# Projecting both halves of v tile by tile, and moving decays, late modulation and weight splits to other steps

## The chip, the cores and the metric

The kernel runs on one NeuronCore of a Trainium2 chip. Its time is in device microseconds (us) for one execution; lower is better. The core has a matmul engine (TensorE, PE in the profile, PEld for its weight loads), VectorE (DVE), ScalarE (ACT), GpSimd (POOL) and a queue engine (SP) that issues most DMA transfers. Every engine executes its own list of instructions in order; semaphores tie the lists together. The matmul engine has two clock levels, 1.2 and 2.4 GHz; the profile gives the granted clock as a share of 2.4 GHz.

## The reference

One layer of a diffusion backbone over 1024 latent tokens and 256 context tokens of width 1024, in float32:

```
sx1, cx1, gx1, sx2, cx2, gx2 = split(silu(c) @ w_mod + b_mod, 6)       # same for the context's first two
hx = rmsnorm(x, norm1) * (1 + cx1) + sx1                                # hc from ctx likewise
u, q, k, v, g, r = split(h @ w_in, [512, 256, 256, 512, 512, 32])       # one projection
lg = log_sigmoid(r @ w_gk2 + b_gk) / 16                                 # per key channel, two directions
o  = chunked gated linear attention(q, k, v, lg), forward + backward, state carried from context
y  = concat(box-window pooling of u @ w_pool, rmsnorm(o) * silu(g)) @ w_out
x  = x + gx1 * y
x  = x + gx2 * moe(rmsnorm(x, norm2) * (1 + cx2) + sx2)                 # 16 experts, top 2, grouped router
return rmsnorm(x, norm_f)
```

The change is in the part that makes u, q, k, v, g and lg; the arithmetic stays as it is.

## The kernel before, in words

Tokens are ten tiles of 128 (tiles 0 to 7 latent, 8 and 9 context). Each float32 matmul of the projection is done as three: every operand is split into a high part (rounded by ScalarE, `part_high`, L659, for weights, `hx_high`, L653, for tokens) and a low part (the difference, by VectorE, `part_low`, L915, and `hx_low`, L911), and high x high, high x low and low x high are summed in PSUM, 24 matmuls for a group (8 blocks of 128 of the width, three products).

The projection is a list of 54 groups, `groups`; all engines walk it in the same loop over n, each doing its share of step n. Before: groups 0 to 9 are v's first 256 columns for tiles 0 to 9, groups 10 to 19 its second 256 columns, 20 to 27 are u, 28 to 33 k, 34 to 37 q, 38 to 45 g's first half, and 46 to 53 g's second half, which run later beside the attention state. The weights are eight parts of 256 columns (m = 0, 1 for v, 2, 3 for u, 4 for k, 5 for q, 6, 7 for g), each with two pieces that are split one after the other. There are two places for a raw part (`raw_part`), one for a high part (`high_part`) and two for a low part (`low_part`). `piece_free` says after which group a piece may be overwritten, `pieces_at` in which step the splits stand.

What TensorE does in step n, in this order: the group (`proj`, L1428 for v and g, L1431 for u, k and q), the eight transposes of tile n+2 (`turn_rows`, L1355), at three steps the low-rank gate projection of several tiles (`rank_rows`, L1401, in `R_STEPS`), the logits of tile n-10 (`logits`, L1446), and the cumulation of the decays of tile n-13 (`cumulate`, L1456). Some steps begin with a matmul against a row of ones (`late_turn`, L1465).

Around it, in step n: ScalarE and VectorE scale the transposed tile n+2 out of PSUM, half each (`hx_out`, L646 and L905), then evacuate group n-1; ScalarE squares rows of a later tile (L632) and does the exponentials and logarithms of the decays (L669 to L684); VectorE scales rows (L898) and does the softplus (L978). The groups of v go in turn to ScalarE (L700) and VectorE (L1029); u and g go to ScalarE, k and q to VectorE (L1038, L1041), multiplied into the decays. v uses two PSUM banks, the other groups four; logits use banks 2 and 3 as the transposes do, so u's groups with four banks wait for softplus.

The late modulation (the four of six vectors that are not needed for hx: 32 quarters of 512 KB of w_mod) is summed on VectorE (`late_sum`, L951 and L953) at the steps in `QUARTERS`; a load goes out when the sum two before it is done. After four quarters TensorE adds over partitions (`late_turn`) and VectorE adds the bias and hands a row of 512 on (`late_row`, L966). The next row's first sum waits for that matmul. SP issues the loads of weight parts and quarters in one written order; a load whose wait is not met holds all behind it.

From step 31 on VectorE also runs the box-window pooling of u (`pool_steps`, L988 to L1019), 32 parts: three a step through step 37, then one a step, and what is left after the loop. Then the state steps of the attention start (L1100, matmuls L1498).

After the loop: state steps with g's second half, scores and output projection, router, and 23 to 24 blocks of the experts (L1644), whose first weight loads wait for the last output projections.

Of the kernel before, what the change touches and what calls it, by code (L numbers as in the profile page):

```python
# [50 lines left out]
LAG_L, LAG_C = 10, 13  # L51
R_STEPS = {3: (0, 4), 7: (4, 4), 9: (8, 2)}
HC = HALF // 2
QUARTERS = ([10 + q for q in range(10)] + [20 + q // 2 for q in range(16)] + [28 + q for q in range(6)])
# [20 lines left out]
def hybrid_block(nc, x, c, ctx_in, c_ctx, w_mod, b_mod, norm1, norm2, w_in, w_gk2, b_gk, w_pool,  # L75
                 pool_scale, gla_gain, w_out, w_router, router_bias, w1, w3, w2, norm_f, inv_counts, out):
    with ExitStack() as stack:
# [47 lines left out]
        ROWS = NT - 1  # L125
        rows_at = [O_Q + t * D for t in range(ROWS)] + [O_V + NX * HALF]
        assert O_Q + ROWS * D == O_V
# [4 lines left out]
        with nc.sbuf_tensor("lead_u", [P, O_U], F32), nc.sbuf_tensor("rank_w", [P, KC, RANK2], F32) as w_r:  # L132
            pass
        sq0 = at(O_U + 256, None, D)
# [130 lines left out]
        groups = ([("v", h, t) for h in range(2) for t in range(NT)] + [("u", p, g) for p in range(NG) for g in range(2)]  # L265
                  + [("k", a, 2) for a in range(2)] + [("k", a, g) for a in range(2) for g in range(2)]
                  + [("q", a, g) for a in range(2) for g in range(2)] + [("g", h, t) for h in range(2) for t in range(NX)])
        NV = 2 * NT
        PB = 4

        def bank_of(n):

            return n % 2 if n < NV else n % PB

        def bank_before(n):

            if n < NV + 2:
                return n - 2
            return {NV + 2: -1, NV + 3: -1}.get(n, n - PB)
# [27 lines left out]

        def piece_free(m, i):

            if by_rows(m) and by_rows(m - 1):  # L310
                return (S["half_used"], m // 4 + 1) if i == 0 else (S["proj_done"], part_end[m - 1])
            if by_rows(m) or by_rows(m - 1):
                return S["proj_done"], part_end[m - 1]
# [3 lines left out]
        for m in range(1, len(parts)):  # L317
            for i in range(2):
                last = part_end[m - 1] if by_rows(m) or by_rows(m - 1) else block_end(m - 1, i)
                pieces_at.setdefault(last - 1, []).append((m, i))  # L320
# [5 lines left out]
        for n, g in enumerate(groups):  # L326
            on_act = g[0] in "ug" or (g[0] == "v" and g[2] % 2 == 0)
# [6 lines left out]
        group_no = {g: n for n, g in enumerate(groups)}  # L334
# [60 lines left out]
        def _(sp):  # L395
# [7 lines left out]
            def load_part(m):  # L403
                if m >= 2:
                    sp.wait_ge(S["proj_done"], part_end[m - 2])
                col = parts[m][1]
                sp.dma_start(raw_part[m % 2].rearrange("p (k n) -> p k n", k=KC), win_v[:, :, col:col + HC]).then_inc(part_loaded[m % 2], 16)
# [15 lines left out]
            for t in range(2, NT):  # L423
                load_rows(t)
            load_part(1)
            for q in range(len(QUARTERS)):
                for m in range(2, 6):
                    if q == {2: 2, 3: 12, 4: 19, 5: 27}[m]:
# [1292 lines left out]
```

## Time and profile before

| | |
|---|---|
| median of 3 runs | 1045.63 us (1043.37 to 1046.85) |
| profiled execution, its own time | 1045.96 us |
| its span, first to last instruction | 1044.2 us |
| mean granted clock of TensorE | 0.929 |
| busy: TensorE, its weight loads | 88%, 71% |
| busy: VectorE, ScalarE, GpSimd | 59%, 37%, 18% |
| stage of the change | about 38 to 320 us of the span |
| instructions | 15159 |

### The profile page before, as it was taken

Reading aid. Unit: us, or ns where it says so; the run is one execution under the profiler, and the core shown is the slowest. Engines: PE = TensorE matmul, PEld = TensorE weight load, DVE = VectorE, ACT = ScalarE, POOL = GpSimd, SP = SyncE. Lnnn points to the kernel's source line nnn. Section 1 sums busy time; section 2 is a strip of 40 time slices with the busy share of each in tenths; the row PEclk is TensorE's granted clock in tenths of the full one; section 3 lists DMA queues with packets and bytes.
Section 4 is the critical chain, followed back from the end, with each engine's and each line's share of the span. In section 5 each row is a group of like instructions: output and inputs, shape, how many; then the busy total and the mean of one; then the engine's idle time right before and its main releaser. Section 6 shows DMA issues by size and latency. Waiting matters only on the chain. (4 is left out here: it accounts for less than half of the span.)

```text
span 1044.2 us, 15159 instructions
## 1 busy us (share of the span) xinstructions
PE 917.3 (88%) x5471; PEld 736.8 (71%) x5472; DVE 616.0 (59%) x814; ACT 388.5 (37%) x525; POOL 189.4 (18%) x210
## 2 busy tenths in 40 slices
PE   3788998899878999999973899999999999999960
PEld 1578776677677845656543788889888888988860
DVE  0554533557995634454436654949975467499933
ACT  1654453210012231212114153737754345477613
POOL 4110000000000001000100122323342232234322
PEclk8888998999989989999995699999999999999985
DMA  9800424552111362111156658898998886699928
GB/s 335 325 2 1 123 88 128 176 180 73 51 41 33 133 239 81 57 65 41 41 193 230 252 147 244 264 323 249 371 380 260 243 266 204 186 339 381 333 38 344
DMA packets 81136, 194.73 MB, mean 186 GB/s; under 512 B 3893, under 2 KB 12218, under 8 KB 81098
## 3 DMA queue, kind: packets, MB, share of 16 engines
q1 hardware_dynamic: 68736, 152.05, 41.4%
q0 software_dynamic: 7616, 25.34, 9.9%
q10 hardware_dynamic: 4746, 16.82, 4.2%
q8 instruction: 25, 0.41, 0.2%
q14 instruction: 13, 0.11, 0.0%
HBM read 168.50 MB, written 25.71 MB: 186 GB/s over the span
## 5 line engine op out<-in xcount | busy, mean ns | idle before, releaser
L1568 PE MATMUL ps<-arena 128*128 128x512 f32 x256 | 113.3, 595 | 0.0
L1644 PE MATMUL ps<-w3h,xTh 128*128 128x256 f32 x368 | 105.9, 288 | 0.0
L1428 PE MATMUL ps<-high,hx_h 128*128 128x256 f32 x288 | 89.0, 309 | 18.7 <-DVE low_even L915 6.7
L1644 PE MATMUL ps<-w3h,xTl 128*128 128x256 f32 x368 | 104.2, 283 | 0.0
L1644 PE MATMUL ps<-w3l,xTh 128*128 128x256 f32 x368 | 104.1, 283 | 0.0
L1428 PE MATMUL ps<-high,hx_l 128*128 128x256 f32 x288 | 85.8, 298 | 0.0
L1568 PEld LDWEIGHTS ps<-arena 128*128 128x128 f32 x256 | 47.4, 190 | 54.4 <-issue 53.6
L1279 DVE TENSOR_TENSOR w1l<-raw,w1h 128x2048 fp32r<-128x2048 f32 x30 | 68.6, 2287 | 29.0 <-ACT w1h L811 29.0
L811 ACT ACTIVATE w1h<-raw 128x2048 fp32r (+1 forms) x32 | 61.1, 1913 | 58.4 <-PE ps L1644 39.4
L1644 PE MATMUL ps<-w2h,hTh 128*128 128x512 f32 x184 | 76.9, 418 | 1.3 <-DVE hTl L1292 0.9
L1428 PEld LDWEIGHTS ps<-high,hx_h 128*128 128x128 f32 x288 | 60.0, 208 | 25.5 <-issue 11.7
L1644 PE MATMUL ps<-w1h,xTh 128*128 128x512 f32 x184 | 72.7, 395 | 3.4 <-DVE xTl L1272 3.4
L1644 PE MATMUL ps<-w1l,xTh 128*128 128x512 f32 x184 | 72.5, 394 | 0.0
L1644 PE MATMUL ps<-w1h,xTl 128*128 128x512 f32 x184 | 72.3, 393 | 0.0
L1644 PE MATMUL ps<-w2l,hTh 128*128 128x512 f32 x184 | 72.2, 392 | 0.0
L1644 PE MATMUL ps<-w2h,hTl 128*128 128x512 f32 x184 | 72.1, 392 | 0.0
L811 ACT ACTIVATE w2h<-raw 128x2048 fp32r (+1 forms) x32 | 61.1, 1918 | 28.9 <-PE ps L1644 21.1
L1279 DVE TENSOR_TENSOR w2l<-raw,w2h 128x2048 fp32r<-128x2048 f32 x32 | 71.7, 2283 | 0.0
L1644 PEld LDWEIGHTS ps<-w3l,xTh 128*128 128x128 f32 x368 | 70.5, 192 | 0.9
L1644 PEld LDWEIGHTS ps<-w3h,xTh 128*128 128x128 f32 x368 | 70.4, 191 | 0.9
L1279 DVE TENSOR_TENSOR w3l<-raw,w3h 128x2048 fp32r<-128x2048 f32 x31 | 70.9, 2286 | 0.0
L1644 PEld LDWEIGHTS ps<-w3h,xTl 128*128 128x128 f32 x368 | 70.5, 192 | 0.0
(259 smaller groups left out, 1961.9 us busy)
## 6 DMA issues: line engine op xcount, KB each, us to landing
raw<-in_w_dram SPq DMA_DIRECT2D x48, 2048.0 KB, 13.5
arena<-in_w_mod_dram SPq DMA_DIRECT2D x32, 512.0 KB, 3.7
arena<-in_w_mod_dram SPq DMA_DIRECT2D x4, 2048.0 KB, 16.0
arena<-in_w_in_dram SPq DMA_DIRECT2D x8, 1024.0 KB, 5.4
x_rows<-arena ACTq DMA_DIRECT2D x9, 512.0 KB, 2.6
hx_rows<-arena ACTq DMA_DIRECT2D x9, 512.0 KB, 2.6
arena<-in_x_dram SPq DMA_DIRECT2D x8, 512.0 KB, 12.6
arena<-in_w_out_dram SPq DMA_DIRECT2D x2, 2048.0 KB, 8.3
```

The lines of the kernel that those rows point to most:

```text
L811: act.activation(half_of(j, w_hi[j][:, :], k), half_of(j, raw[:, bass.ds(base, UNIT)], k), ACT.Copy).then_inc(w_high[j], 1)
L1279: dve.tensor_tensor(half_of(j, w_lo[j][:, :], k), half_of(j, raw[:, bass.ds(base, UNIT)], k), half_of(j, w_hi[j][:, :], k).bitcast(F32), A ...
L1428: ins = pe.matmul(out_ap, hx[x_][:, t, k, :], w[w_][:, k, :], start=(k == 0 and i == 0), stop=(k == KC - 1 and i == 2))
L1568: ins = pe.matmul(ps[:, 5 + h, :], m, w[:, k, :], start=(k == 0), stop=(k == KC - 1))
L1644: ins = pe.matmul(out_ap, parts[l][:, lhs], w_parts[w][:, cols], start=start and n == 0, stop=stop and n == 2)
```

## The change

- v's groups run tile by tile: group 2t is the first half of tile t, group 2t+1 the second. The high part of v's second weights has its own place (`high_v1`, over what is later part of the queries' decays), so both are split before the loop; one for q's weights too (`high_q`), and a third place for raw weights is used for u's first part.
- The transposes of tile t+2 stand behind group 2t (tile 2's behind group 1). Scaling, squares and rows move with them. All of v is evacuated by ScalarE.
- Logits stand at steps 15 to 24, cumulations at 17 to 26 (before 10 to 19 and 13 to 22); rank matmuls behind groups 7, 15 and 18.
- Late modulation: one quarter a step from 4 to 19, two a step from 20 to 27, none later; `late_turn` stands behind the step's group (8, 12, 16, 20, 22, 24, 26, 28) and `late_row` at the end of VectorE's step.
- v and u together use two banks, k, q and g four. Pooling starts at step 30. The splits of g's first part stand in step 35, in q, and VectorE's splits stand ahead of its sums and its pooling.
- SP: rows 2, v's second part, rows 3 to 9, the last two each behind a transpose, then quarters with u's and k's parts among them, then q's and g's.

```diff
--- before.py
+++ after.py
...
 COL_U, COL_Q, COL_V, COL_G, COL_R = 0, HALF, HALF + 2 * QK, 2 * HALF + 2 * QK, 3 * HALF + 2 * QK
-LAG_L, LAG_C = 10, 13
-R_STEPS = {3: (0, 4), 7: (4, 4), 9: (8, 2)}
+LAG_L, LAG_C = 15, 17
+R_STEPS = {7: (0, 4), 15: (4, 4), 18: (8, 2)}
 HC = HALF // 2
-QUARTERS = ([10 + q for q in range(10)] + [20 + q // 2 for q in range(16)] + [28 + q for q in range(6)])
+QUARTERS = ([4 + q for q in range(16)] + [20 + q // 2 for q in range(16)])
 MID = P // 2
...
-        ROWS = NT - 1
-        rows_at = [O_Q + t * D for t in range(ROWS)] + [O_V + NX * HALF]
-        assert O_Q + ROWS * D == O_V
+        rows_at = [O_K + 3 * D, O_K + 4 * D, O_Q, O_Q + D, O_K, O_K + D, O_K + 2 * D, O_V + NX * HALF]
+        rows_at += rows_at[0:2]
+        assert O_K + 5 * D == O_V
         rows = [at(off, None, D) for off in rows_at]
             pass
+        with nc.sbuf_tensor("lead_v1", [P, O_Q + 4 * HALF], F32), nc.sbuf_tensor("high_v1", [P, PART], F32R) as high_v1:
+            pass
+        with nc.sbuf_tensor("lead_q", [P, O_G], F32), nc.sbuf_tensor("high_q", [P, PART], F32R) as high_q:
+            pass
+        raw_u0 = at(O_U + 256, None, PART)
+        high_of = {1: high_v1, 5: high_q}
         sq0 = at(O_U + 256, None, D)
...
         FIN_GROUPS = [(0, 1), (1, 1), (2, 2), (4, 2), (6, 2)]
-        groups = ([("v", h, t) for h in range(2) for t in range(NT)] + [("u", p, g) for p in range(NG) for g in range(2)]
+        groups = ([("v", h, t) for t in range(NT) for h in range(2)] + [("u", p, g) for p in range(NG) for g in range(2)]
                   + [("k", a, 2) for a in range(2)] + [("k", a, g) for a in range(2) for g in range(2)]
         NV = 2 * NT
+        group_no = {g: n for n, g in enumerate(groups)}
         PB = 4
+        RING = NV + 2 * NG
-            return n % 2 if n < NV else n % PB
+            return n % 2 if n < RING else n % PB
-            if n < NV + 2:
-                return n - 2
-            return {NV + 2: -1, NV + 3: -1}.get(n, n - PB)
+            return n - 2 if n < RING + 2 else {RING + 2: -1, RING + 3: -1}.get(n, n - PB)
...
+        def high_for(m):
+
+            return high_of.get(m, high_part)
+
+        def raw_for(m):
+
+            return raw_u0 if m == 2 else raw_part[m % 2]
+
         def piece_free(m, i):
-            if by_rows(m) and by_rows(m - 1):
-                return (S["half_used"], m // 4 + 1) if i == 0 else (S["proj_done"], part_end[m - 1])
-            if by_rows(m) or by_rows(m - 1):
-                return S["proj_done"], part_end[m - 1]
+            if m == 7:
+                return (S["half_used"], 1) if i == 0 else (S["proj_done"], part_end[6])
+            if m in (2, 6):
+                return S["proj_done"], part_end[m - 2]
+            if m == 5:
+                return S["proj_done"], group_no[("k", 1, 0)]
             return S["proj_done"], block_end(m - 1, i)
         pieces_at = {}
-        for m in range(1, len(parts)):
+        for m in range(2, len(parts)):
             for i in range(2):
-                last = part_end[m - 1] if by_rows(m) or by_rows(m - 1) else block_end(m - 1, i)
-                pieces_at.setdefault(last - 1, []).append((m, i))
+                step = {2: part_end[0] - 1, 5: group_no[("k", 1, 0)] + i, 6: group_no[("q", 0, 1)], 7: part_end[6] - 1}.get(m)
+                pieces_at.setdefault(block_end(m - 1, i) - 1 if step is None else step, []).append((m, i))
+
+        turn_after = {1: 2, **{2 * (t - 2): t for t in range(3, NT)}}
+        hx_at = {n + 1: t for n, t in turn_after.items()}
+        scale_at = {2 * (t - 2) - 1: t for t in range(3, NT)}
+        square_at = {2 * (t - 2) - 3: t for t in range(4, NT)}
         for n, g in enumerate(groups):
-            on_act = g[0] in "ug" or (g[0] == "v" and g[2] % 2 == 0)
+            on_act = g[0] in "ugv"
             if on_act:
                 evac[n] = ("ev_v", nv)
-        group_no = {g: n for n, g in enumerate(groups)}
...
             def load_part(m):
-                if m >= 2:
+                if m == 2:
+                    sp.wait_ge(S["mod_turned"], 1)
+                    sp.wait_ge(S["ss_ready"], NT)
+                elif m >= 3:
                     sp.wait_ge(S["proj_done"], part_end[m - 2])
                 col = parts[m][1]
-                sp.dma_start(raw_part[m % 2].rearrange("p (k n) -> p k n", k=KC), win_v[:, :, col:col + HC]).then_inc(part_loaded[m % 2], 16)
+                sp.dma_start(raw_for(m).rearrange("p (k n) -> p k n", k=KC), win_v[:, :, col:col + HC]).then_inc(part_loaded[m % 2], 16)
...
             load_part(0)
-            for t in range(2, NT):
+            load_rows(2)
+            load_part(1)
+            for t in range(3, NT):
+                if t >= 8:
+                    sp.wait_ge(S["turned"], t - 7)
                 load_rows(t)
-            load_part(1)
             for q in range(len(QUARTERS)):
-                for m in range(2, 6):
-                    if q == {2: 2, 3: 12, 4: 19, 5: 27}[m]:
+                for m in range(2, 5):
+                    if q == {2: 11, 3: 18, 4: 26}[m]:
                         load_part(m)
                 load_late(q)
+            load_part(5)
             load_part(6)
...
                 act.wait_ge(part_loaded[m % 2], 16 * (m // 2 + 1))
-                if m >= 1:
+                if m >= 2:
                     act.wait_ge(*piece_free(m, i))
-                act.activation(piece(high_part[:, :], m, i), piece(raw_part[m % 2], m, i), ACT.Copy).then_inc(S["part_high"], 1)
+                act.activation(piece(high_for(m)[:, :], m, i), piece(raw_for(m), m, i), ACT.Copy).then_inc(S["part_high"], 1)
...
                 elif g[0] == "u":
+                    if g[1:] == (2, 0):
+                        act.wait_ge(S["lg_done"], NT)
                     out_ap, func = uT[:, g[1], g[2] * HALF:(g[2] + 1) * HALF], ACT.Copy
...
             part_high(0, 1)
-            square(2)
             hx_out(1)
             hx_high(1)
+            square(2)
+            part_high(1, 0)
+            part_high(1, 1)
             square(3)
             for n in range(group_no[("g", 1, 0)]):
-                if n + 2 < NT:
-                    hx_out(n + 2)
+                if n in hx_at:
+                    hx_out(hx_at[n])
                 if n >= 1:
                     evacuate(n - 1)
-                if n + 2 < NT:
-                    hx_high(n + 2)
-                if n + 4 < NT:
-                    square(n + 4)
+                if n in hx_at:
+                    hx_high(hx_at[n])
+                if n in square_at:
+                    square(square_at[n])
                 if 0 <= n - LAG_C - 1 < NT:
...
                 dve.wait_ge(S["part_high"], 2 * m + i + 1)
-                dve.tensor_tensor(piece(low_part[m % 2][:, :], m, i), piece(raw_part[m % 2], m, i),
-                                  piece(high_part[:, :], m, i).bitcast(F32), ALU.subtract).then_inc(S["part_split"], 1)
+                dve.tensor_tensor(piece(low_part[m % 2][:, :], m, i), piece(raw_for(m), m, i),
+                                  piece(high_for(m)[:, :], m, i).bitcast(F32), ALU.subtract).then_inc(S["part_split"], 1)
...
             part_low(0, 1)
-            scale_rows(2)
             hx_out(1)
             hx_low(1)
+            part_low(1, 0)
+            part_low(1, 1)
+            scale_rows(2)
             sc = ("s_chain", [0])
...
                 for c in range(count):
-                    dve.tensor_copy(rT[0:32, (first + c) * P:(first + c + 1) * P], ps[RANK2 * c:RANK2 * (c + 1), 6, 0:P])\
+                    dve.tensor_copy(rT[0:32, (first + c) * P:(first + c + 1) * P], ps[RANK2 * c:RANK2 * (c + 1), 4, 0:P])\
                         .then_inc(S["rT_ready"], 1)
...
             pooling = pool_steps()
-            pool_from = group_no[("k", 1, 2)] + 2
+            pool_from = group_no[("k", 1, 2)] + 1
             for n in range(group_no[("g", 1, 0)]):
-                if n + 2 < NT:
-                    hx_out(n + 2)
+                if n in hx_at:
+                    hx_out(hx_at[n])
                 if n - 1 in R_STEPS:
                     evacuate(n - 1)
-                if n + 3 < NT:
-                    scale_rows(n + 3)
-                if n + 2 < NT:
-                    hx_low(n + 2)
+                if n in scale_at:
+                    scale_rows(scale_at[n])
+                if n in hx_at:
+                    hx_low(hx_at[n])
                 if 0 <= n - LAG_C < NT:
                     softplus(n - LAG_C)
-                if n - 1 in late_turn_at:
-                    late_row(late_turn_at[n - 1])
+                for m, i in pieces_at.get(n, ()):
+                    part_low(m, i)
                 for q, at_step in enumerate(QUARTERS):
                         next(pooling, None)
-                for m, i in pieces_at.get(n, ()):
-                    part_low(m, i)
+                if n - 1 in late_turn_at:
+                    late_row(late_turn_at[n - 1])
             for _ in pooling:
...
-                if n == 3:
+                if n == 7:
                     pe.wait_ge(S["rw_loaded"], 16)
...
                         for c in range(count):
-                            ins = pe.matmul(ps[RANK2 * c:RANK2 * (c + 1), 6, 0:P], w_r[:, k, :],
+                            ins = pe.matmul(ps[RANK2 * c:RANK2 * (c + 1), 4, 0:P], w_r[:, k, :],
                                             hx[part][:, first + c, k, :].bitcast(F32), start=(k == 0 and part == 0),
...
                 elif n >= NV:
-                    pe.wait_ge(S["sp_ready"], n - NV + 7)
-                w = [p_[:, :].rearrange("p (k n) -> p k n", k=KC) for p_ in (high_part, low_part[m % 2])]
+                    pe.wait_ge(S["sp_ready"], NT)
+                w = [p_[:, :].rearrange("p (k n) -> p k n", k=KC) for p_ in (high_for(m), low_part[m % 2])]
                 if g[0] == "v" and g[1] == 0:
...
                                             start=(k == 0 and i == 0), stop=(k == KC - 1 and i == 2))
-                    if k == 3 and n + 1 == part_end[m] and m in (0, 6):
+                    if k == 3 and n + 1 == part_end[m] and m == 6:
                         ins.then_inc(S["half_used"], 1)
...
             for n in range(group_no[("g", 1, 0)]):
+                proj(n)
+                if n in turn_after:
+                    turn_rows(turn_after[n])
                 if n in late_turn_at:
                     late_turn(late_turn_at[n])
-                proj(n)
-                if n + 2 < NT:
-                    turn_rows(n + 2)
                 if n in R_STEPS:
```

## Rows read from the trace of the kernel before

**Rows 1.** The page, busy us, share of the span, instructions.

```profile
PE 917.3 (88%) x5471; PEld 736.8 (71%) x5472; DVE 616.0 (59%) x814; ACT 388.5 (37%) x525; POOL 189.4 (18%) x210
```

**Rows 2.** Stretches: us, length, TensorE busy (instructions), mean clock, DMA share, GB/s.

```profile
45.60:98.20 52.60, 41.07 (x480) 0.87 0.06 20
98.20:104.20 6.00, 6.00 (x56) 1.00 0.00 0
104.20:165.80 61.60, 53.17 (x375) 0.97 0.41 120
165.80:203.50 37.70, 37.65 (x158) 0.91 0.44 134
203.50:266.00 62.50, 52.40 (x226) 0.94 0.45 139
266.00:289.10 23.10, 23.09 (x96) 0.95 0.04 12
289.10:320.20 31.10, 24.45 (x192) 0.89 0.11 35
320.20:335.40 15.20, 11.19 (x94) 0.89 0.00 0
```

**Rows 3.** TensorE's waits: line, releaser, us, times, longest; four stretches in turn.

```profile
PE ps L1428 <- DVE arena L1029: 6.6, 3, 3.1
PE ps L1428 <- ACT arena L700: 3.9, 2, 1.9
PE ps L1428 <- DVE hx_l L911: 1.1, 1, 1.1
...
PE ps L1446 <- DVE arena L978: 8.5, 4, 4.9
...
PE ps L1465 <- DVEq L958: 10.1, 4, 3.3
...
PE ps L1428 <- DVE low_even L915: 6.7, 1, 6.7
PE ps L1498 <- DVE state L1100: 2.5, 1, 2.5
```

**Rows 4.** Timeline around 40 to 45 us: start, duration, engine, instruction, count.

```profile
40.21 1.22 DVE L915 TENSOR_TENSOR low_even<-arena,high 128x1024 fp32r<-128x1024 f32 x1
...
42.81 1.36 DVE L905 TENSOR_SCALAR hx_f<-ps,a,mod 128x128 f32<-128x128 f32 x4
...
41.06 1.50 ACT L646 ACTIVATE hx_f<-ps,mod,a 128x128 f32<-128x128 f32 x4
...
44.47 1.04 PE L1355 MATMUL ps<-ident,arena 128*128 128x128 f32 x8
```

**Rows 5.** Groups by line, 38 to 170 us: count, busy us, mean ns, idle before.

```profile
L953 DVE SCALAR_TENSOR_TENSOR wp<-arena,silu_c,wp 128x512 f32<-128x512 f32 x21 | 15.7, 748 | 0.7 <-DVE wp L953 0.2
...
L659 ACT ACTIVATE high<-arena 128x1024 fp32r<-128x1024 f32 x5 | 5.2, 1049 | 1.5 <-PE ps L1428 1.5
```

**Rows 6.** Groups by line of VectorE, 237 to 330 us: the pooling.

```profile
L995 DVE TENSOR_TENSOR arena<-arena 128x1024 f32<-128x1024 f32 (+6 forms) x10 | 15.3, 1531 | 0.5 <-DVE wp L953 0.2
L1011 DVE TENSOR_TENSOR arena<-arena 128x1024 f32<-128x1024 f32 (+6 forms) x10 | 13.0, 1300 | 0.4
...
L1004 DVE TENSOR_TENSOR arena<-arena,icnt 128x1024 f32<-128x1024 f32 x4 | 4.9, 1226 | 0.1
```

**Rows 7.** Stretch 260 to 300: busy PE, PEld, DVE, ACT, POOL, then clock and DMA.

```profile
260.00:300.00 40.00, 30.04 (x128) 23.72 (x127) 38.12 (x49) 4.34 (x4) 1.41 (x2) 0.87 0.19 60
```

**Rows 8.** Timeline of VectorE: the first state step.

```profile
328.16 1.13 DVE L1100 TENSOR_SCALAR state<-ps,dec 128x128 f32<-128x128 f32 x4
```

**Rows 9.** DMA issues: count, size of one, median us from issue to landing.

```profile
arena<-in_w_mod_dram SPq DMA_DIRECT2D x32, 512.0 KB, 3.7
arena<-in_w_mod_dram SPq DMA_DIRECT2D x4, 2048.0 KB, 16.0
arena<-in_w_in_dram SPq DMA_DIRECT2D x8, 1024.0 KB, 5.4
```

## The prediction

> **What bounds the kernel now.** I read the page's busy line first: TensorE is busy 88% of the span and no other engine over 60% [rows 1]. So what can shrink is TensorE's idle time and the time it runs at the lower clock. The diff touches only the projection loop, some 45 to 320 us, so next comes the table of stretches of that loop. In it the reader is to see that the first stretch (v's first half, 45.6 to 98.2) is busy 41.1 of 52.6 us at a mean clock of 0.87, and that the stretch of g's first half (289 to 320) is busy 24.5 of 31.1 us; the clean row is the second: two groups of v in 6.0 us at clock 1.00 [rows 2]. Third come TensorE's waits: 11.6 us in v's first half, all between a tile's transposes and the next group; 8.5 us for softplus in v's second half; 10.1 us for the late modulation sum in u and k; 6.7 us for the weights of g; 2.5 us for the first state step [rows 3]. Together 39.4 us.
>
> The clock takes the rest. A row's mean clock is a mix of 1.2 and 2.4 GHz; one minus it, times the busy time, is about what the lower level cost. Over the stretches without the clean one [rows 2]: 0.13 x 41.1 = 5.3; 0.03 x 53.2 = 1.6; 0.09 x 37.7 = 3.4; 0.06 x 52.4 = 3.1; 0.05 x 23.1 = 1.2; 0.11 x 24.5 = 2.7; 0.11 x 11.2 = 1.2. Sum 18.5 us.
>
> So 57.9 us of this loop and of the first state step are not matmul at full clock. TensorE's instructions stay the same in number and shape, so the change can win only from these 57.9 us, and it must be charged with each new wait. What comes after needs all tokens (router, then experts), and the experts' first loads wait for the last output projections, so I pass all of it on to the end.
>
> **Part by part.** I follow the new order by durations of one operation: a v group 3.0 us [rows 2], a u, k or q group of 512 columns 5.6 us (four in 23.1 us at clock 0.95), a tile's eight transposes 1.0 us [rows 4], a split into high 1.05 us on ScalarE and into low 1.2 us on VectorE, one step of a late sum 0.75 us, so 1.5 us for a quarter [rows 4, 5].
>
> *Transposes two tiles ahead, two groups a tile.* Before, transposes of tile t+2 were followed at once by the group that needed, through its bank, ScalarE's or VectorE's evacuation queued behind the scaling of that same tile. Now after the transposes of a tile come one group, two at most, that need nothing of it. Scaling (1.5 us, ScalarE) [rows 4] and the short evacuation behind it end some 2 us after the transposes, the next group takes 3.0: the 11.6 us go, with a margin of 1 us. VectorE's budget is tighter: per tile 1.4 (its half of the scaling), under 1.2 for the rows, 1.2 (low part), two quarters of a late sum 3.0, so at most 6.8 us against TensorE's 3.0 + 3.0 + 1.0 = 7.0. What hides it is that a tile's scaling is due only 6 us after its transposes end. At groups 8, 12 and 16 the sum waits for TensorE's own row of ones, which puts VectorE 2.5 us back; I take 0.2 us for that. With its cover gone it costs what is over: 1 us a tile.
>
> *Price of it at the start.* Group 1 now needs v's second half of the weights. VectorE ends the first half at 41.4, then scales tile 1 (1.4, to 42.8); ScalarE makes its high part (1.1, to 43.9), squares tile 2 (1.2, a pass like a split and a short read), splits the weights (1.05, to 46.1); VectorE subtracts (1.2): 47.3. TensorE ends group 0 at 44.6 [rows 4], so 2.7 us of waiting. All seven waits of 2.5 us or more that I followed on the timeline had a spell of the lower clock behind them; I charge 1.5 us a spell (5.3 us over the four spells of v's first half, rounded up) [rows 2, 3]. Sum 4.2.
>
> *Decays run in u.* Logits of a tile are now two steps ahead of its softplus and VectorE has no evacuation of v before it, so the softplus is ready a group earlier: 3.6 of the 8.5 us go. The other 4.9 us stood before u, where the splits of u's weights waited for the last v group. Now u's weights need only the first half's last group: one v group, the rank matmuls and some decays lie over 2 x 1.05 + 1.2 us. They go. In return five logits and seven cumulations of decays run between u groups; the count is the same. SP's queue: v's second half is now ahead of seven row loads (1 MB, some 3 us), hidden, since row 3 is due about 50 us; rows 8 and 9 wait for transposes 0 and 1, done by 40 us. u's first load comes between late quarters 10 and 11, with four groups before it is due, against 5.4 us of landing [rows 9].
>
> *Late modulation ahead of k.* A quarter's load is issued when the sum two before it is done, and lands in 3.7 us [rows 9]: a pair of quarters needs 5.2 us, two v groups take 6 to 7, a u step 7. It holds. TensorE's matmul for a row stands after the group instead of ahead of it, which gives VectorE 5.6 us more. In u I find each row ready 0.5 to 2.5 us before TensorE comes. The last is not: between u's last group and the row at group 28 lie 1.05 + 1.2 (k's second piece), two quarters 3.0 and the row's own add 0.7, in all some 6.2 with handoffs, under a group of 3.0. A wait of 3.2 us, and a spell of clock 1.5: 4.7 charged, of the 10.1 us that go.
>
> *Extra places.* g's weights are split during q (its load is issued after the last k group, 5.4 + 2 x 1.05 + 2 x 1.2 = 10 us, against 22 of q). The 6.7 us go. But VectorE: pooling's parts now start one step earlier, 24 of 32 by the end of q instead of 21. The operations of pooling sum to some 50 us (15.3 + 13.0 + 3 x 4.9, three lines being alike, and some 7 of copies, memsets and chaining) [rows 6], of which 39 are now due before q's last evacuation, with nine evacuations (11) and four splits (4.8): 55.2 us from the end of group 29. TensorE does eight groups (44.8) and three of g (8.7), then wants that bank: at 53.5. A wait of 1.7 us, and half a spell: 2.5. If TensorE is slower elsewhere this wait shrinks; if VectorE's chain is 5% longer it is 4.5.
>
> *First state step.* VectorE began it at 328.2, some 7.7 us after group 45, with three parts of pooling (5.2 us) behind the last split [rows 8]. Now one part (2.5 us) is left, so it starts 2.7 us sooner: the 2.5 us go, to the last tenth.
>
> **The sum.** 57.9 removed; added 4.2 + 0.2 + 4.7 + 2.5 = 11.6; 46.3 us. I keep back 3 us for handoffs where I found under 1.5 us of margin (some eight places). So 43 us from the profiled execution's 1045.96: 1003 us. That execution lies 0.3 us above the median shown (1045.63), which I ignore.
>
> From both sides: the new waits could be nil (the 11.6 and the 3 come back: 988) or, by the nearest rows, each as long as the longest of its kind (4.9 for VectorE, 6.7 for the weights, 3.3 for the sum, with spells: 19): 1011.
>
> One rule of the Trainium skill speaks against the change. u had four PSUM banks and now has two. The trace has v in two banks with no wait between groups and clock 1.00 in the clean stretch [rows 2]. *TensorE: Matmul & The Clock Gate*, section "A second HAM failure mode: psum-queue depth-cycling", says that cycling through PSUM banks leaves micro-idles that make the clock swing between its two levels. By the row it costs nothing. By the rule the clock of the whole loop would stay as it was, which is the rival below.
>
> **Rivals.**
> A. The clock stays low in v and u though the waits go. For: v's first half lost 5.3 us to the clock though, by the longest of each kind, its waits were mostly under 2 us [rows 2, 3]. Against: 1.00 in the clean row. Then only 0 to 4 of the 18.5 us come back: 1003 + 15 to 18 = 1018 to 1021.
> B. VectorE becomes the bound in v and again in k and q. For: it was busy 38 of 40 us around q before [rows 7]. Against: its budget of 6.8 a tile is just under TensorE's. Price: 1 us for each of eight tiles, and 3 more at group 41: 1003 + 11 = 1014.
> C. Slower: the late sums set the pace of v. They now stand in VectorE's queue between one tile's scaling and the next, with two places for their input. If a quarter's load takes longer than 5 us (3.4 a step, twice, less 1.5), every further us delays a pair of steps by one; the sixteen quarters beside v would have to cost 43 us, so landings of over 10 us each. Landings of 16 us are there only for the 2 MB loads at the start; the median of these is 3.7 [rows 9]. Then about 1055.
> D. The change doesn't reach the end: what is won before the experts is waited for there. For: experts' weights are DMA-heavy. Against: their loads start from the output projection, not from a clock. Then 1025 to 1043.
>
> **Chances.** Forecast with its own range 993 to 1011: 0.70. A 0.12, B 0.10, C 0.03, D 0.04, and 0.01 that it is faster than 993. The range that should hold 8 of 10 reaches through B and most of A: 992 to 1020. A measurement of this kernel tells 0.3% (3 us) from no change. Faster 0.96, same 0.01, slower 0.03.
>
> **What would show it.** TensorE's waits behind transposes gone; one of some 3 us before group 1; none before u and before g; one of some 3 us at the row matmul after k's first group; one of 1 to 3 us at the fourth g group; u's first group starting near 134 us instead of 169.6, and g's first half ending near 275 to 278 instead of 320. The mean clock of v's stretch at 0.95 or more; if it is below 0.9, A. If VectorE's idle time in v is nil, B. If sums wait for their loads by more than 10 us in v, C. If the loop ends 40 us earlier and the kernel does not, D. My figure is wrong if a wait stands where I found margins: softplus at groups 16 to 24, or the rows' sums in u.

## The result, and the profile after

The changed kernel takes 1000.07 us (median of 4 runs, 998.54 to 1002.27) against 1044.62 us before in the same comparison: ratio 0.9573, 95% interval 0.9546 to 0.9599, so 44.5 us or 4.3% faster. The forecast was 1003 us, its range 992 to 1020. The profiled execution took 1000.63 us, its span is 998.8 us, 45.4 less than before; mean granted clock 0.941 (before 0.929). TensorE has the same 5471 matmuls:

```profile
PE 904.7 (91%) x5471; PEld 726.8 (73%) x5472; DVE 612.5 (61%) x804; ACT 391.3 (39%) x535; POOL 190.7 (19%) x210
```

The stretches of the loop, cut where the stages now lie (us, length, TensorE busy and instructions, mean clock, DMA share, GB/s). They answer to [rows 2]: v's groups 2 to 19 are the second, u the third, the first k groups the fourth, the rest of k and q the fifth, g's first half the sixth.

```profile
48.00:53.40 5.40, 5.33 (x33) 0.68 0.03 10
53.40:135.70 82.30, 81.02 (x851) 1.00 0.38 113
135.70:196.50 60.80, 60.41 (x270) 1.00 0.51 157
196.50:210.00 13.50, 9.64 (x53) 0.75 0.38 117
210.00:253.30 43.30, 43.30 (x193) 1.00 0.08 25
253.30:279.00 25.70, 23.34 (x194) 1.00 0.14 42
279.00:294.50 15.50, 13.97 (x139) 1.00 0.20 65
```

v now runs at 1.00 with 1.3 us of waiting where its first half alone had 11.6 us and a clock of 0.87. u's first group starts at 135.7 us (forecast 134, before 169.6). Low clock is left in two places, each right behind a wait: 0.32 x 5.33 = 1.7 us and 0.25 x 9.64 = 2.4 us, 4.1 in all against 18.5 before.

TensorE's waits (line, releaser, us, times, longest), 45 to 135 us and then 135 to 330 us; they answer to [rows 3]. L1461 is `proj` for v and g, L1498 the row matmul, L1531 the state's matmul, L1562 comes after the loop:

```profile
PE ps L1461 <- DVE low_odd L946: 2.1, 1, 2.1
PE ps L1498 <- DVEq L991: 1.3, 1, 1.3
...
PE ps L1498 <- DVE state L999: 4.2, 2, 3.9
PE ps L1461 <- DVE arena L1074: 2.4, 1, 2.4
PE ps L1562 <- issue: 1.7, 1, 1.7
PE ps L1531 <- ACT ktok L768: 1.5, 1, 1.5
PE ps L1531 <- DVE state L1130: 0.8, 1, 0.8
```

Those of the loop (the first four) sum to 10.0 us; before, 39.4 with the first state step. The first state step no longer waits: VectorE does it at 284.2, 5.1 us after g's first half ended at 279.1, before 7.7 us after (VectorE's timeline, start and duration; answers to [rows 8]).

```profile
284.16 1.13 DVE L1133 TENSOR_SCALAR state<-ps,dec 128x128 f32<-128x128 f32 x4
```

So 29.4 us of waits and 14.4 us of clock, 43.8 us of the 45.4, lie in that ledger. By the third state step the changed kernel is 45.5 us ahead (290.0 against 335.5), though its group 0 started 0.8 us later (41.1 against 40.3), and it is 45.4 ahead at the end. So nothing is lost or won in the experts, and the loop itself gained 46.3 us, of which 2.5 are not in the ledger; what they are is not shown.

### The profile page after: what moved, and what is told of

The parts are those of the page before. It is cut to its first block and busy times, and to the rows that moved or that the text cites. A ratio compares the mean times of both kernels' runs of the same rounds, so it can differ in the third digit from the quotient of the medians.

```text
span 998.8 us, 15160 instructions
## 1 busy us (share of the span) xinstructions
PE 904.7 (91%) x5471; PEld 726.8 (73%) x5472; DVE 612.5 (61%) x804; ACT 391.3 (39%) x535; POOL 190.7 (19%) x210
## 3 DMA queue, kind: packets, MB, share of 16 engines
q1 hardware_dynamic: 68736, 152.05, 43.3%
## 5 line engine op out<-in xcount | busy, mean ns | idle before, releaser
L842 ACT ACTIVATE w3h<-raw 128x2048 fp32r (+1 forms) x32 | 61.3, 1917 | 22.4 <-PE ps L1677 19.2
L1461 PE MATMUL ps<-high,hx_h 128*128 128x256 f32 x208 | 60.9, 293 | 2.7 <-DVE arena L1074 2.4
L591 POOL COPY block_tok<-slot_tok 128x1 int32 (+1 forms) x24 | 25.1, 1048 | 179.9 <-PE ps L1671 147.9
```

Of the source, the lines that this page charges most:

```text
L591: pool.tensor_copy(block_tok[:, :], slot_tok[:, bass.ds(b, 1)]).then_inc(S["tok_ready"], 1)
L842: act.activation(half_of(j, w_hi[j][:, :], k), half_of(j, raw[:, bass.ds(base, UNIT)], k), ACT.Copy).then_inc(w_high[j], 1)
L1461: ins = pe.matmul(out_ap, hx[x_][:, t, k, :], w[w_][:, k, :], start=(k == 0 and i == 0), stop=(k == KC - 1 and i == 2))
```

## The experiments

A ratio compares a kernel's runs with runs of the kernel before that were timed beside them, with a 95% interval; a time is the median of the kernel's runs. The stage ahead of the loop ended up to 2.7 us apart between profiled executions (group 0 starts between 40.0 and 42.7 us), so effects under 3 us are read from the waits of the loop, not from the medians.

**One part alone: evacuation ahead of scaling.** The kernel before, with the evacuation moved up on ScalarE (shown) and in the same way on VectorE, where it then also stands ahead of the copy of the rank rows:

```diff
             for n in range(group_no[("g", 1, 0)]):
+                if n >= 1:
+                    evacuate(n - 1)
                 if n + 2 < NT:
                     hx_out(n + 2)
-                if n >= 1:
-                    evacuate(n - 1)
```

> The kernel before, with one thing changed: in each step ScalarE and VectorE evacuate the last group ahead of scaling the new tile instead of behind it. Theory 1 (the waits in v's first half are the evacuation queued behind the scaling): of 11.6 us under 3 stay, and some of the 5.3 us of low clock: 10 to 14 us faster than before, 1031 to 1035. Theory 2 (scaling, high part and low part in a row are the bound of a tile): waits stay near 11 us, within 3 us of before.

Measured 1031.8 us, ratio 0.9871 (0.9837 to 0.9904): 12 to 14 us faster. TensorE's waits and its stretch, 45 to 96 us:

```profile
PE ps L1428 <- DVE hx_l L911: 1.2, 1, 1.2
PE ps L1428 <- DVE arena L1029: 0.6, 2, 0.4
PE ps L1355 <- DVE arena L898: 0.4, 1, 0.4
...
45.00:96.00 51.00, 48.77 (x621) 1.00 0.16 49
```

Theory 1: 2.2 us of the 11.6 are left, and the clock of this stretch is 1.00. It holds more matmuls than the first of [rows 2]; the same 480 now lie between 45.4 and 82.4 us, with TensorE busy 34.9 of 37.0 us at a clock of 1.00 instead of 0.87. The low clock went with the waits. For these 480 the time is 15.6 us shorter (37.0 against 52.6) and the whole span 13.4, so some 2 us are lost again further on; of these the waits for the late sums show 0.8 (10.9 against 10.1). Scaling, high part and low part in a row are no bound at one group a tile.

**All orders, none of the places.** The kernel before with that swap and:

```diff
-LAG_L, LAG_C = 10, 13
+LAG_L, LAG_C = 10, 12
...
-                if n - 1 in late_turn_at:
-                    late_row(late_turn_at[n - 1])
+                for m, i in pieces_at.get(n, ()):
+                    part_low(m, i)
                 for q, at_step in enumerate(QUARTERS):
...
-                for m, i in pieces_at.get(n, ()):
-                    part_low(m, i)
+                if n - 1 in late_turn_at:
+                    late_row(late_turn_at[n - 1])
...
-                if n in late_turn_at:
-                    late_turn(late_turn_at[n])
                 proj(n)
                 if n + 2 < NT:
                     turn_rows(n + 2)
+                if n in late_turn_at:
+                    late_turn(late_turn_at[n])
```

> The kernel before with orders and one lag changed, and none of the changed kernel's order of groups or extra places: evacuation ahead of scaling, VectorE's weight splits ahead of its sums and its pooling, the row matmul behind the group and the row's add at the end of the step, cumulation 12 steps behind in place of 13. Theory 1 (the gain is the order of instructions in each queue): 12 us as measured for the evacuation, some 7 of the 8.5 for softplus, 7 of the 10.1 for the sums, 4 of the 6.7 before g, with clock 30 to 36 us faster than before, 1008 to 1014. Theory 2 (tile by tile and the extra places are what carries it): under 20 us faster, 1024 or more.

Measured 1021.4 us, ratio 0.9768 (0.9733 to 0.9802): 23 us faster, between the two theories, half of the whole change. TensorE's waits, 45 to 320 us:

```profile
PE ps L1465 <- DVEq L958: 7.2, 2, 4.4
PE ps L1428 <- DVE low_even L915: 6.0, 1, 6.0
PE ps L1498 <- DVE state L1100: 3.9, 1, 3.9
PE ps L1465 <- DVE state L966: 3.9, 1, 3.9
PE ps L1498 <- ACT ktok L737: 1.5, 1, 1.5
PE ps L1428 <- DVE hx_l L911: 1.0, 1, 1.0
PE ps L1431 <- DVE low_even L915: 0.7, 1, 0.7
...
```

The softplus wait of 8.5 us is gone whole. The rest of theory 1 failed: the sums and their row wait 11.1 us (7.2 and 3.9) where 10.1 stood before and some 3 were expected, g's weights 6.0 where 6.7 stood and some 2.7 were expected. The 7.2 lie in k and q (at 214.0 and 244.3 us), beside whose evacuations and pooling VectorE does its sums; the 3.9 lie in u (184.1). Before g, VectorE begins the split at 268.0 us, though ScalarE began its part at 263.5: pooling and an evacuation of q stand ahead of it. So the swap and the end of the softplus wait account for this gain; b_evacfirst, the swap alone, still had the 8.5 us. In the waits for the sums and for g's weights, on the old order of groups, the three other moves show next to no gain. What the new order of groups and the new steps bring is probably room, with sixteen quarters beside a longer v and none beside k; that is argued from these waits and not shown by a run of its own.

**Softplus one step later.** The changed kernel with a distance of three steps between logits and cumulation, as before:

```diff
-LAG_L, LAG_C = 15, 17
+LAG_L, LAG_C = 15, 18
```

> The changed kernel, with cumulation and softplus one step later (lags 15 and 18 in place of 15 and 17), so that a tile's logits need a softplus that stands in VectorE's next step, as before the change. Theory 1 (this one step is what took the softplus waits away): logits wait at groups 16 and 20 to 24 behind the late sums and the splits, 2 to 6 us each, in all 15 to 25 us slower, 1015 to 1025. Theory 2 (what took them away is that v is no longer evacuated by VectorE): 0 to 4 us slower.

Measured 1043.25 us, ratio 0.9985 (0.9966 to 1.0005): the whole gain is gone. Theory 1 in its mechanism, but its figure of 15 to 25 us is missed: the loss is 43. TensorE's wait for it (45 to 330 us), its stretch of v's end and u (110 to 240 us), and VectorE at one of these waits (timeline):

```profile
PE ps L1479 <- DVE arena L1011: 30.5, 7, 7.3
...
110.00:240.00 130.00, 99.13 (x455) 0.83 0.32 93
```

```profile
161.04 1.23 DVE L946 TENSOR_TENSOR low_odd<-arena,high 128x1024 fp32r<-128x1024 f32 x1 [11.82 <-ACT high L686]
162.18 3.22 DVE L986 SCALAR_TENSOR_TENSOR wp<-arena,silu_c,wp 128x512 f32<-128x512 f32 x4
165.75 0.68 DVE L999 TENSOR_TENSOR state<-ps,ktok 1x512 f32<-1x512 f32 x1 [0.35 <-DVE wp L986]
166.35 0.67 DVE L1011 SCALAR_TENSOR_TENSOR arena<-ps,arena 128x512 f32<-128x512 f32 x1
```

The softplus that TensorE wants right behind its group (L1011) stands a step later in VectorE's queue, behind a weight split (L946) whose high part ScalarE (L686) makes only when that same group has ended, two quarters of a late sum (3.2 us) and the row's add: 7.3 us, with TensorE's next matmul at 167.2. VectorE is idle 11.8 us ahead of the split. A wait of 7.3 us stands there twice; at three u steps where the row matmul lies between it is 4.1 us. The 30.5 us brought the clock of the stretch down to 0.83, which is 0.17 x 99.1 = 17 us more at most.

**Both lags later.** The control to it:

```diff
-LAG_L, LAG_C = 15, 17
+LAG_L, LAG_C = 16, 18
```

> The changed kernel with both lags one step later (16 and 18 in place of 15 and 17). Theory 1 (the distance of two steps between logits and cumulation is what counts, since u_lag with distance three lost 43 us): within 2 us of the changed kernel. Theory 2 (u has no room for the decays, so any step later costs): 10 us slower or more.

Measured 1001.65 us, ratio 0.9578 (0.9543 to 0.9614), not to be told from the changed kernel: theory 1. What counts is the distance, two steps instead of three, and not the place. The trace has one new wait of 2.2 us, of a cumulation for ScalarE's exponentials.

**v on VectorE again.**

```diff
-            on_act = g[0] in "ugv"
+            on_act = g[0] in "ug" or (g[0] == "v" and g[2] % 2 == 0)
```

> The changed kernel with v's odd tiles evacuated by VectorE again, as before. Theory 1 (VectorE's budget of a tile is just under TensorE's, and the evacuation ties it to TensorE's pace): waits in v of 2 to 6 us, 2 to 8 us slower. Theory 2 (VectorE has room in v, the order does the work): within 1 us.

Measured 999.24 us, ratio 0.9567 (0.9535 to 0.9599): theory 2. One wait of 1.3 us for an evacuation stands in v, in place of the one of 1.3 at the row matmul. VectorE was not near its bound in v.

**Late modulation at the old steps.**

```diff
-QUARTERS = ([4 + q for q in range(16)] + [20 + q // 2 for q in range(16)])
+QUARTERS = ([10 + q for q in range(10)] + [20 + q // 2 for q in range(16)] + [28 + q for q in range(6)])
...
-                for m in range(2, 5):
-                    if q == {2: 11, 3: 18, 4: 26}[m]:
+                for m in range(2, 6):
+                    if q == {2: 2, 3: 12, 4: 19, 5: 27}[m]:
...
-            load_part(5)
```

> The changed kernel, with the late modulation at the steps of before (10 to 33) and SP's order to match; the row matmul still stands behind the group. Theory 1 (being ahead of k is what matters): the 10.1 us of waits for the sums come back, 8 to 12 us slower. Theory 2 (standing behind the group is what matters, and the steps only trade places): the 3.9 us wait after k's first group goes, and VectorE's six more quarters in k (4.6 us) lengthen the wait at the fourth g group from 2.4 to 6 to 8 us: between 2 us faster and 3 us slower.

Measured 1013.5 us, ratio 0.9698 (0.9661 to 0.9735), 13 us slower than the changed kernel by the ratios: just above theory 1's 8 to 12 us. TensorE's waits from 45 to 292 us, and VectorE's late sum at 97 us (timeline):

```profile
PE ps L1497 <- DVEq L990: 7.8, 3, 2.9
PE ps L1460 <- DVE arena L1073: 6.4, 2, 4.4
PE ps L1460 <- DVE low_odd L945: 2.6, 1, 2.6
PE ps L1387 <- DVE arena L928: 2.2, 1, 2.2
```

```profile
97.10 1.54 DVE L985 SCALAR_TENSOR_TENSOR wp<-arena,silu_c,wp 128x512 f32<-128x512 f32 x2 [5.32 <-DMA arena<-in_w_mod_dram]
```

The waits of the loop sum to 19.0 us against 10.0, and the clock from 45 to 292 us is 0.96, which costs some 9 us against 4.1. The row matmul waits 7.8 us in all where the changed kernel has 5.5 (1.3 and 4.2), and the six quarters in k lengthen the wait for q's evacuation (L1073) from 2.4 to 6.4, as theory 2 had it. Not all of it is k: 4.5 us of the waits stand in v (2.2 at a tile's transposes and 2.3 at the row matmul). They follow the late sum shown, for whose quarter VectorE waits 5.3 us: in SP's order of this kernel that load stands behind the load of u's first part, which SP held back until 90.2 us. So the run shows that the steps of the quarters, with the order of loads that goes with them, are worth 13 us; how much of that is k alone is not separated.

**g's first weights split after q.** The extra place for q's high part makes it possible to split g's inside q. Undone:

```diff
-            if m in (2, 6):
-                return S["proj_done"], part_end[m - 2]
+            if m == 2:
+                return S["proj_done"], part_end[0]
+            if m == 6:
+                return S["proj_done"], part_end[5]
...
-                step = {... 6: group_no[("q", 0, 1)], 7: part_end[6] - 1}.get(m)
+                step = {... 6: part_end[5] - 1, 7: part_end[6] - 1}.get(m)
```

> The changed kernel, with g's first weights split only after q's last group, as before. Theory 1 (the early place for the split is worth the wait that stood there): the 6.7 us wait before g and its low clock return, so about 8 us slower than the changed kernel, 1008. Theory 2 (VectorE is the bound from q into g, so the split only changes where TensorE waits for it): one wait of some 4 us before g, the wait of 2.4 us at the fourth g group goes, 1 to 3 us slower, 1002.

Measured 1000.98 us, ratio 0.9575 (0.9542 to 0.9609): as the changed kernel. A wait of 2.6 us stands before g, and that of 2.4 at the fourth g group is gone: theory 2, at the low end of its cost. Then, with VectorE's split also put behind the pooling of its step:

```diff
                 for m, i in pieces_at.get(n, ()):
-                    part_low(m, i)
+                    if m < 6:
+                        part_low(m, i)
...
                         next(pooling, None)
+                for m, i in pieces_at.get(n, ()):
+                    if m >= 6:
+                        part_low(m, i)
```

> The changed kernel with g's first weights split after q (as in u_gsplit) and in addition VectorE's splits of g's weights behind the pooling of their step, as before. u_gsplit was within 1 us of the changed kernel. Theory 1 (what took the 6.7 us away is that the split now stands ahead of pooling): a wait of 8 to 10 us before g, 7 to 9 us slower, 1008. Theory 2 (the order on VectorE is indifferent too): within 1 us.

Measured 1008.2 us, ratio 0.9645 (0.9615 to 0.9676), 7 us slower than u_gsplit: theory 1. TensorE's wait before g in u_gsplit and in this kernel (190 to 320 us):

```profile
PE ps L1463 <- DVE low_even L948: 2.6, 1, 2.6
```

```profile
PE ps L1467 <- DVE low_even L948: 8.7, 1, 8.7
```

**The terms that I had charged, taken back one by one.** The last row matmul behind group 30; two parts of pooling a step from q's second group (step 35) on, in q instead of three and in g instead of one; v's first four groups in another order:

```diff
-        late_turn_at = {QUARTERS[4 * i + 3] + 1: i for i in range(8)}
+        late_turn_at = {QUARTERS[4 * i + 3] + (3 if i == 7 else 1): i for i in range(8)}
```

```diff
-                    for _ in range(3 if n < group_no[("g", 0, 0)] else 1):
+                    for _ in range(3 if n < group_no[("q", 0, 1)] else 2):
```

```diff
-        groups = ([("v", h, t) for t in range(NT) for h in range(2)] + ...
+        groups = ([("v", h, t) for h in range(2) for t in range(2)] + [("v", h, t) for t in range(2, NT) for h in range(2)] + ...
```

> The changed kernel, with the last row matmul of the late modulation behind group 30 instead of group 28. The trace after has 3.9 us of waiting there and a spell of the lower clock behind it (0.8 us in the row matmul, 1.7 us in the next group). Theory 1 (that wait is TensorE's own loss): 6.4 us go and 1.7 us come back at the fourth g group, since VectorE begins its evacuations of k no earlier than its last sums allow and adds the row among them: 4 to 6 us faster than the changed kernel. Theory 2 (VectorE is the bound from the sums to g): all of it comes back at the fourth g group, within 1 us of the changed kernel.

Measured 994.77 us, ratio 0.9533 (0.9513 to 0.9554), some 4 us under the changed kernel by the ratios. The wait of 3.9 us is gone; the stretch behind it is at full clock, and the wait at the fourth g group stays at 2.2 us:

```profile
PE ps L1461 <- DVE arena L1074: 2.2, 1, 2.2
PE ps L1498 <- DVE state L999: 0.4, 1, 0.4
...
196.50:210.00 13.50, 13.50 (x81) 1.00 0.35 113
```

Theory 1, in size too (4 to 6 us); by the trace nothing came back at the fourth g group, where 1.7 were expected.

> The changed kernel, with three parts of pooling a step only up to q's second group and two a step from there, so that two fewer stand ahead of q's last evacuation each step. Theory 1 (the wait at the fourth g group is pooling queued ahead of q's evacuation): 2.4 us and its 0.3 us of clock go and nothing comes back at the first state step, 2 to 3 us faster. Theory 2 (VectorE has too much to do up to the state steps): the wait moves to the first state step, within 1 us.

Measured 997.08 us, ratio 0.9555 (0.9528 to 0.9581). No wait is left between 205 and 276 us, and none came to the first state step; by the trace theory 1. By the ratios it is 2 us faster, not to be told from nothing. Its trace has a new wait of 2.5 us after the loop (L1551 for ScalarE, at 323.1 us), which f_all, with the same edit, does not have (0.2).

> The changed kernel, with v's first four groups in the order first half of tile 0, first half of tile 1, second half of tile 0, second half of tile 1. Theory 1 (group 1 waits for the split of v's second weights): the wait of 2.1 us falls under 0.5 and the low clock over group 1 (1.5 us) may go: 1.5 to 3.5 us faster. Theory 2 (tile 1 is no earlier than those weights, since both stand behind one another on ScalarE and VectorE): wait of 1.5 us or more, within 1 us.

Measured 999.33 us, ratio 0.9572 (0.9552 to 0.9592). TensorE's waits from 42 to 60 us, and the stretch from group 0 on, in this kernel:

```profile
PE ps L1388 <- DVE arena L929: 0.8, 1, 0.8
PE ps L1461 <- DVE hx_l L942: 0.4, 1, 0.4
...
42.70:55.00 12.30, 11.49 (x78) 0.84 0.47 173
```

The same stretch in the changed kernel:

```profile
41.10:53.60 12.50, 10.38 (x58) 0.71 0.57 220
```

0.4 us of waiting is left for the group and 0.8 is new for the transposes, whose rows VectorE scales behind the splits: 1.2 instead of 2.1, with 20 matmuls more done in the stretch, at 0.84 instead of 0.71. The low clock that is left lies in group 0. By the trace of the waits that is theory 1; but its 1.5 to 3.5 us are not there: the median is 0.7 us lower and the ratio the same. Group 0 itself started 1.6 us later in this execution (42.7 against 41.1). A gain in time isn't shown.

> The three together. If the terms add: 4.7 + 2.6 + 2.5, about 10 us faster than the changed kernel, 990. If VectorE is the bound from the last sums into g, only the start and the pooling count: 995.

Measured 988.17 us, ratio 0.9471 (0.9447 to 0.9495), clear of the changed kernel's interval and 11 to 12 us under it, by the ratios and by the medians: what was forecast if the terms add (10). The three alone came to 6 us by their ratios and 9 by their medians, each known only to some 2 or 3 us. TensorE from the second group to the end of g's first half:

```profile
45.40:268.90 223.50, 219.50 (x1584) 1.00 0.35 106
```

In the loop little is left for reordering: the whole stretch is at full clock with some 3 us of waits.

## Why the prediction was right, step by step

- *What bounds.* Right: 57.9 us were waits and low clock, and 43.8 of them went, where 43.3 were forecast; the rest of the kernel passed on what was won by the third state step to 0.1 us. That the time came out so near is in part luck: 2.5 us of the gain stand in no term.
- *Transposes two tiles ahead.* The waits went. The cause named (evacuation queued behind the scaling) is shown by the swap alone. The budget of 6.8 us a tile for VectorE was too high: VectorE is busy 41.4 of 56.6 us between 53.4 and 110, and giving it back half of v costs nothing. Rival B in v is refuted.
- *Price at the start.* 2.7 us were forecast and 2.1 measured, with 1.7 us of low clock behind them where 1.5 was charged.
- *Decays in u.* Right: no softplus wait is left. The prediction gave two reasons, the shorter distance and VectorE's freedom from v's evacuations. The first is the one that holds (u_lag, u_vdve), and it said nothing of how much hangs on it: with a step more, 43 us are lost.
- *Late modulation.* At group 28 a wait of 3.2 us was forecast and 3.9 measured, with 2.4 us of clock for 1.5. At group 12 it was 1.3 for 0.2.
- *Extra places.* The sum was right, the reason incomplete. I let the 6.7 us before g go because the split could be made during q. It could have stayed after q at no cost in time: 2.6 us then stand before g and 2.4 go at the fourth g group. What must not come back is VectorE's split behind the pooling of its step (8.7 us). That order is not enough by itself either, for in b_order, with it, 6.0 us stayed. The early split with VectorE's old order was not tried. The wait of 1.7 us charged at the fourth g group was 2.4, with the clock of the stretch behind it at 1.00, where 0.8 was charged.
- *First state step.* Right: 2.6 us sooner, wait gone. In b_order the wait grew to 3.9 us: there the last weight split (at 294.9 us) stands ahead of pooling that ran on to 304.0, and the state followed at 304.3.
- *Rival A.* Refuted: u with two PSUM banks runs 60.4 of 60.8 us at 1.00 [rows 2 had 0.91 to 0.94]. The rule of the Trainium skill (*TensorE: Matmul & The Clock Gate*, "A second HAM failure mode: psum-queue depth-cycling") does not come into play in this trace: it speaks of short idle times between groups, and with two banks u has 0.4 us of idle time in all.
- *Rivals C and D.* In the changed kernel no load of a quarter set the pace: in v VectorE never waits for one, in u 2.2 us in all. In u_quarters one did, for 5.3 us. Nothing was given back in the experts.
- *The 3 us kept back.* The ledger's new waits and clock came to 10.0 + 4.1 = 14.1 us, where I had 11.6 + 3. The excess of 2.5 lies in terms that I had named (group 28 with 1.6, group 12 with 1.1), and not in handoffs elsewhere.

## What to carry to other kernels

Where engines work through their queues in order, count for each wait how many steps apart producer and consumer stand, and what in between waits for the consumer's own engine: here one step too many made a loop in which both engines wait for each other, and cost 43 us, as much as the whole change had won. Before giving memory to a tensor so that work can start earlier, try moving that work ahead of what needn't be ready yet; here 23 us, half of the gain, came without any new place, from five moved calls and one lag. And charge a wait with the clock that may fall behind it.

## What the runs showed that I had not expected

Waits of TensorE can be dearer than they look. With 30.5 us of softplus waits, v's end and u ran at a mean clock of 0.83. In the swap on the kernel before, a stretch of the same 480 matmuls rose from 0.87 to 1.00 when its waits fell from 11.6 to 2.2 us. Behind the wait of 2.1 us the changed kernel's group took 4.6 us where one at full clock takes 3.1; in f_all the same place has a wait of 0.2 us and its group took 3.1.

But not every wait has that price. In the changed kernel those of 1.3 us (at 96.7) and of 2.4 us (at 264.4) have a clock of 1.00 in the stretch behind them. In the kernel before, two waits of 1.8 us differ: the 6 us behind the one at 59.9 us have a mean clock of 0.72, those behind the one at 90.7 us 1.00. So 1.5 us a wait is a price to plan with, not a rule.
